# Two ends of a transformer kernel: inputs and modulation in halves ahead of the first product, and the last layer norm done with tokens on the partitions

## The chip, the cores and the metric

The kernel runs on one core of one Trainium2 chip. The metric is the device time of one execution in microseconds (us); the median of three runs stands for the kernel. The core has five engines with a queue each: TensorE (PE; its weight loads are shown as PEld), VectorE (DVE), ScalarE (ACT), GpSimd (POOL) and SyncE (SP), which issues all DMAs here. Data lies in SBUF with 128 partitions; PE writes to PSUM, eight banks of 128 x 512 f32.

## What is computed

One token sequence (512 tokens, 1024 features) goes through three layers. The first and the last of their parts matter here:

```python
mod = silu(c) @ w_mod + b_mod                    # 3 x 1024: shift, scale, gate
u = rms_norm(x, norm_w) * (1 + scale) + shift    # x: 512 x 1024
uc = rms_norm(ctx, norm_w) * (1 + scale_c) + shift_c   # 256 context tokens
p = u @ w_in                                     # then attention, conv, w_out
...
y = (silu(h @ w_gate) * (h @ w_up)) @ w_down     # 2816 wide
x = layer_norm(ALPHA * x + (1 + g_f) * y, ln_ffn_g, ln_ffn_b)   # the output
```

In between come two blocks with other attentions and two feed-forward parts. Everything is f32; the large products split both operands into a high part (F32R) and a low part and take three F32R matmuls instead of one f32 matmul.

## The kernel before

Every engine has its program written out by hand, and semaphores join them. The residual stream `xT` has features on the partitions: eight tiles of 128 features x 512 tokens. Weights come in chunks of 1 MB (`load_chunk`, two slots of `wraw`); ACT makes the high part (`split_high`, line 1453), DVE the low part (`split_low`, line 1952), and PE takes 16 blocks times three matmuls per chunk (`product`, lines 797 to 799). A chunk is loaded once the low part of the chunk two before is done.

**The prologue.** SP issues 15 small vectors, then the modulation weights of group 0 (four loads of 512 KB, called ticks), `x` (four loads), the context (1 MB), group 1, chunk 0, groups 2 and 3, nine small tables and chunk 1 (lines 486 to 515). A group is 512 columns of `w_mod`: groups 0 and 1 are the shift, groups 2 and 3 the scale. The 16 ticks go through four slots of `mfirst`; a load waits until PE has used the tick four before (line 480). PE multiplies each tick with the silu of the condition (`tick`, line 727), ACT copies a finished group to SBUF (`copy_group`, line 1461), PE transposes it (`turn_group`, line 740) and DVE adds the bias (`group_columns`, line 1960). PE also transposes `x` to `xT` (`input_tile`, tiles 0 to 7, line 762) and the normalized `x` (tiles 8 to 15). ACT makes the squares (line 1474), the root (line 1478) and the scaled copies (line 1482). When all four groups are there, DVE computes the scales (line 1985), splits chunk 0, and modulates tile by tile (line 1995); ACT makes the high part (line 1465) and DVE the low part (line 1968) of each. PE enters product 0 only behind the transposes of tile 15, and its k-th step waits for the k-th low part. Behind products 0, 1 and 2 PE transposes eight context tiles, and `ticks_of` puts two ticks of the next group behind each product; the group's turn lies in the middle of a later one (`TURN_AT`). On ACT the high parts of the context tiles come before `copy_group` (lines 1532 to 1535).

**The tail.** The last down projection has four column groups (j) of three chunks (c). DVE adds each finished pair of tiles to `xT` (`add_out`, line 2583). Mean and mean square come from matmuls with a matrix of 1/1024 (`moments`, lines 1223 to 1229), so they stand on all partitions at once; ACT squares tiles 4 to 7 late, and POOL sums (`far_half`). Then ACT copies the mean to SBUF (line 1758), DVE and POOL subtract it from the eight tiles (lines 2663 and 648), DVE and ACT compute the variance and its root (lines 2662, 1775, 1777), DVE multiplies the eight tiles (line 2670), ACT applies gain and bias (line 1788), PE transposes 32 blocks to PSUM (line 1426), DVE and ACT copy half token tiles to SBUF (lines 2878 and 1937), and SP stores them in eight DMAs of 256 KB (line 561).

Of the kernel before, what the change touches and what calls it, by code (L numbers as in the profile page):

```python
# [76 lines left out]
QUERY_AT = {5: 0, 6: 1, 7: 2, 8: 3}  # L77

# [66 lines left out]
def program(nc, t, out):  # L145
    ctx = ExitStack()
    with ctx:
# [8 lines left out]
        with ExitStack() as o:  # L156
# [80 lines left out]
        ln_pre, ln_m4, ln_sh, ln_pair, ln_six, ln_row, ln_v, ln_far, half_done = [sem(n) for n in (  # L237
            "ln_pre", "ln_m4", "ln_sh", "ln_pair", "ln_six", "ln_row", "ln_v", "ln_far", "half_done")]
# [8 lines left out]
        out_tile = sem("out_tile")  # L247
        fin_T, fin_v, fin_a = sem("fin_T"), sem("fin_v"), sem("fin_a")
# [207 lines left out]

        block = ctx.enter_context(nc.Block())
# [3 lines left out]
        def _(sp):  # L461
# [36 lines left out]
            for tt in range(TT):  # L498
                sp.dma_start(xtok[:, tt], t["x"][0, tt * P:tt * P + P, :]).then_inc(x_in, 16)
            sp.dma_start(ctok[:, :, :], t["ctx"][0].rearrange("(t p) n -> p t n", p=P)).then_inc(ctx_in, 16)  # L500
            for g in range(1, 4):
                for kp in range(4):
                    load_tick(g, kp)
                if g == 3:
                    sp.dma_start(ropet[:, 0], t["cos1"].rearrange("(t p) n -> p t n", p=P)).then_inc(tab_in, 16)
                    sp.dma_start(ropet[:, 1], t["sin1"].rearrange("(t p) n -> p t n", p=P)).then_inc(tab_in, 16)
                    sp.dma_start(qkw[:, 0], t["q_norm_w"].to_broadcast([P, HD])).then_inc(tab_in, 16)
                    for tt in range(TT):
                        sp.dma_start(posi[:, tt:tt + 1], t["positions_2"][0, tt * P:tt * P + P]
                                     .rearrange("(p o) -> p o", o=1)).then_inc(tab_in, 16)  # L510
                    sp.dma_start(ifr[:, :], t["inv2"].to_broadcast([P, 32])).then_inc(tab_in, 16)
                    sp.dma_start(qkw[:, 1], t["k_norm_w"].to_broadcast([P, HD])).then_inc(tab_in, 16)
                    load_chunk(1)
                if g == 1:
                    load_chunk(0)
# [37 lines left out]
            for n in range(N_DN[1], NCH - 2):  # L553
                load_chunk(n + 2)
            for i in range(2 * TT):
                tt, half = i % 4, i // 4
                if i < 6:
                    sp.wait_ge(fin_v, i + 1)
                else:
                    sp.wait_ge(fin_a, i - 5)  # L560
# [6 lines left out]
        def _(pool):  # L567
# [61 lines left out]
            def far_half(L, a):  # L629
# [70 lines left out]
        def _(pe):  # L700
# [45 lines left out]
            def input_tile(f):  # L746
# [4 lines left out]
                if f == 8:  # L751
                    pe.wait_ge(xn_rd, 4)
                if f == 16:
                    pe.wait_ge(xn_rd, 6)
# [10 lines left out]
            first_tiles = (range(0, 8), (), range(8, 11), ())  # L765
            for g in range(4):
                for kp in range(4):
                    tick(g, kp)
                if g >= 1:
                    turn_group(g - 1)  # L770
                for f in first_tiles[g]:
                    input_tile(f)
            turn_group(3)
            for f in range(11, 16):
                input_tile(f)

            def product(n, a, nk, u0, xh, xl, w_hi, w_lo, turn=None, k0=0, first=True, done=True, ready=u_lo, near=None, ends=None, mid=None):
# [8 lines left out]
                for i, (m, k) in enumerate(steps):  # L786
# [443 lines left out]

            def out_product(L, l, n0):
# [11 lines left out]
            def feed_forward(l):  # L1243
# [38 lines left out]
                moments(2 * l + 1, A_DN[l] + 3)  # L1282
# [140 lines left out]
            for k in range(KT):  # L1423
                pe.wait_ge(ax_rd, 32 + k + 1)
                for tt in range(TT):
                    last = tr(ps[:, 2 * tt + k // 4, (k % 4) * P:(k % 4) * P + P], xT[:, k, tt * P:tt * P + P], ident[:])
                    if k % 4 == 3:
                        last.then_inc(fin_T, 1)


        @block.scalar
        def _(act):
# [36 lines left out]
            act.wait_ge(ctx_in, 16)  # L1469
# [5 lines left out]
            copy_group(0)  # L1475
# [4 lines left out]
            for tt in range(6):  # L1480
                src = xtok[:, tt] if tt < 4 else ctok[:, tt - 4]
                A(xn[:, tt] if tt < 4 else ctok[:, tt - 4], src, ACT.Copy, scale=rstd[:, tt:tt + 1]).then_inc(xn_rd, 1)
            for g in range(1, 3):
                copy_group(g)
            split_high(0)
            copy_group(3)
            for i in range(8):
                high(U_U + i, uH[:, i])
            split_high(1)
# [9 lines left out]
            for n in range(N_PW):  # L1499
# [253 lines left out]
            def mean_row(L):  # L1753
                act.wait_ge(ln_mean, L + 1)
                if L < 3:
                    A(spare(L, 3), X[:, 0, :], ACT.Square).then_inc(ln_row, 1)
                else:
                    A(spare(L, 1), X[:, 0, :], ACT.Copy).then_inc(ln_row, 1)
# [13 lines left out]
            def norm(L, n):  # L1772
                rs = X[:, 2, :] if L < 3 else tmp[:, 0]
# [4 lines left out]
                if L < 3:  # L1778
                    for x in range(8):
                        i = U_LN[L] + x  # L1780
                        act.wait_ge(u_tmp, i + 1)
                        A(uH[:, x], tmp[:, i % 2], ACT.Identity, bias=fcol[:, L, 1, x:x + 1]).then_inc(u_hi, 1)  # L1782
                        if x == 2:
                            act.wait_ge(chunk_done, n - 1)
                            split_high(n)
                for x in range(8):
                    act.wait_ge(ln_t, 16 * L + x + (5 if L == 3 else 9))
# [8 lines left out]
            def feed_forward(l):  # L1796
# [15 lines left out]
                for n in range(N_DN[l], N_DN[l] + 12):  # L1812
                    L, a = 2 * l + 1, A_DN[l] + 3
                    if n == N_DN[l] + 11:
                        nc.scalar.preload_act_table_set(LOG_EXP)
                        squares(L, a, (6, 7))
                        mean_row(L)
# [8 lines left out]
                norm(2 * l + 1, N_ODD + 1)  # L1826
# [108 lines left out]
            for tt in range(2, TT):  # L1935
                act.wait_ge(fin_T, 4 + tt + 1)
                A(otok[:, tt, 512:D], ps[:, 2 * tt + 1, :], ACT.Copy).then_inc(fin_a, 1)


        @block.vector  # L1940
        def _(dve):
# [13 lines left out]
            def group_columns(g):  # L1955
                dve.wait_ge(modT, g + 1)
                if g < 6:
                    o, b = mod1[:, 4 * g:4 * g + 4, :], cols[:, VBM + 4 * g:VBM + 4 * g + 4]
# [17 lines left out]
            V.reciprocal(rstd, rstd).then_inc(rin_rd, 1)  # L1976
            dve.wait_ge(cols_rd, 1)
            for g in range(2):
                group_columns(g)
            for g in range(2, 4):  # L1980
                group_columns(g)
            dve.wait_ge(mod_rd, 4)

            for c, dst in ((0, scS), (1, scC)):
                V.scalar_tensor_tensor(dst, mod1[:, 8:16, c], 1.0, cols[:, VNW:VNW + 8], ALU.add, ALU.mult)\
                    .then_inc(sc_rd, 1)
            split_low(0)
            dve.wait_ge(sc_rd, 2)
# [9 lines left out]
            for i in range(8):  # L1998
                modulate(i)
                if i >= 1:  # L2000
# [654 lines left out]
            def last_norm(L):  # L2655
                row, sq, var = spare(L, 1), spare(L, 3), spare(L, 2)
                dve.wait_ge(ln_row, L + 1)
                link(V.tensor_tensor(sq, row, row, ALU.mult))
                for x in range(4):
                    if x == 1:  # L2660
                        dve.wait_ge(ln_var, L + 1)
                        V.tensor_tensor(var, X[:, 1, :], sq, ALU.subtract).then_inc(ln_v, 1)
                    V.tensor_tensor(xT[:, x], xT[:, x], row, ALU.subtract).then_inc(ln_t, 1)
                dve.wait_ge(ln_rs, 2 * L + 2)
                for x in range(8):
                    if x < 4:
# [248 lines left out]
```

## Time and profile before

| what | value |
|---|---|
| median of 3 runs (lowest, highest) | 1800.19 us (1798.35, 1802.16) |
| the profiled execution's own time | 1807.2 us |
| its span in the trace | 1805.5 us |
| mean granted clock of PE | 0.964 of full |
| busy share of PE, DVE, ACT, POOL | 93%, 56%, 37%, 19% |

Matmuls are pipelined and their ends are modelled, so two of them overlap in the rows; the distance from start to start is what one takes in a row of its kind. A row of the timeline that says x4 has merged four neighbours. An f32 matmul stands as two passes.

### The profile page before, as it was taken

To read this page: it belongs to the slowest core of one execution; us is meant where nothing else is said; L and a number is where in the kernel's file an instruction comes from. 1 tells how busy PE (TensorE), PEld (TensorE's weight loads), DVE (VectorE), ACT (ScalarE), POOL (GpSimd) and SP (SyncE) were. 2 spreads that over 40 slices of the span, in tenths; PEclk is the share of its full clock that TensorE was granted. 3 is DMA by queue.
4 is the path that set the end of the run, shared out by engine and by line. 5 is a ranking of instruction groups with operands and counts; after the bars stand their busy time and mean duration, and the time that the engine had idled before them with its cause. 6 is when DMAs were issued, how large, how long until landed. Compare 5 with 4: busy or idle time off the path is not lost.

```text
span 1805.5 us, 22686 instructions
## 1 busy us (share of the span) xinstructions
PE 1677.7 (93%) x8899; PEld 1371.9 (76%) x8905; DVE 1017.3 (56%) x1430; ACT 665.1 (37%) x896; POOL 341.7 (19%) x264
## 2 busy tenths in 40 slices
PE   4899999999998998999999999899979899999996
PEld 3698787888776876788887876677758688888875
DVE  1558798677879657633333246756675733333244
ACT  4313465443353433433332223434453533333123
POOL 0000000000000002688885011224311100000012
PEclk8899999999998899999999999999989999999999
DMA  8535300242222233466664222212002223322221
GB/s 287 181 107 172 104 25 1 88 163 94 94 82 82 70 94 117 140 185 186 186 186 134 87 95 85 82 59 71 24 24 71 68 95 102 106 93 87 87 82 47
DMA packets 145349, 187.08 MB, mean 104 GB/s; under 512 B 6893, under 2 KB 104533, under 8 KB 145268
## 3 DMA queue, kind: packets, MB, share of 16 engines
q1 hardware_dynamic: 145268, 185.96, 32.4%
q8 instruction: 55, 0.90, 0.2%
q14 instruction: 26, 0.21, 0.0%
HBM read 183.85 MB, written 2.10 MB: 103 GB/s over the span
## 4 chain that ended last, share of the span: by engine, by line
PE 58%; DVE 16%; POOL 9%; issue 7%; DMA 5%; ACT 4%; SPq 0%; another core or an unknown queue 0%; POOLq 0%; DVEq 0%; ACTq 0%
PE ps L797 7%; PE ps L799 7%; PE ps L798 7%; POOL mraw L598 4%; POOL msum L605 4%; DMA mraw<-in_w_mod_dram 3%; PE ps L1260 2%; PE ps L1267 2%; PE ps L1261 2%; PE ps L1268 2%; PE ps L1264 2%; PE ps L1269 2%; PE ps L1315 2%; PE ps L1317 2%; PE ps L1316 2%
## 5 line engine op out<-in xcount | busy, mean ns | idle before, releaser
L1453 ACT ACTIVATE whi<-wraw 128x2048 fp32r<-128x2048 f32 x71 | 135.8, 1913 | 313.4 <-PE ps L799 231.6
L1952 DVE TENSOR_TENSOR wlo<-wraw,whi 128x2048 fp32r<-128x2048 f32 x64 | 148.9, 2327 | 174.4 <-ACT whi L1453 174.2
L2689 DVE TENSOR_TENSOR wlo<-wraw,whi 128x2048 fp32r<-128x2048 f32 x22 | 51.6, 2347 | 203.4 <-ACT whi L1804 203.4
L1260 PE MATMUL ps<-uH,whi 128*128 128x512 f32 x352 | 141.0, 401 | 10.6 <-ACT uH L1782 8.3
L797 PE MATMUL ps<-hH,whi 128*128 128x512 f32 x352 | 141.2, 401 | 0.0
L798 PE MATMUL ps<-hL,whi 128*128 128x512 f32 x352 | 140.0, 398 | 0.0
L799 PE MATMUL ps<-hH,wlo 128*128 128x512 f32 x352 | 140.0, 398 | 0.0
L1261 PE MATMUL ps<-uH,wlo 128*128 128x512 f32 x352 | 139.4, 396 | 0.0
L1268 PE MATMUL ps<-uL,whi 128*128 128x512 f32 x352 | 136.9, 389 | 0.0
L1269 PE MATMUL ps<-uH,wlo 128*128 128x512 f32 x352 | 136.9, 389 | 0.0
L1267 PE MATMUL ps<-uH,whi 128*128 128x512 f32 x352 | 136.9, 389 | 0.0
L1264 PE MATMUL ps<-uL,whi 128*128 128x512 f32 x352 | 111.0, 397 | 3.9 <-DVE uL L2630 3.9
L605 POOL TENSOR_TENSOR msum<-msum,mraw 128x512 f32<-128x512 f32 x66 | 107.6, 1630 | 5.2
L797 PE MATMUL ps<-uH,whi 128*128 128x512 f32 x256 | 103.3, 403 | 0.0
L798 PE MATMUL ps<-uL,whi 128*128 128x512 f32 x256 | 100.7, 393 | 0.0
L799 PE MATMUL ps<-uH,wlo 128*128 128x512 f32 x256 | 100.7, 393 | 0.0
L598 POOL TENSOR_TENSOR mraw<-mraw,cpad 128x1024 f32<-128x1024 f32 x44 | 84.2, 1912 | 56.5 <-PE ps L734 43.7
L1808 ACT ACTIVATE whi<-wraw 128x2048 fp32r<-128x2048 f32 x22 | 42.2, 1920 | 137.3 <-PE ps L1269 137.3
L1801 ACT ACT_TABLE_LOAD x22 | 28.2, 1283 | 173.3 <-PE ps L1264 173.3
L2012 DVE SCALAR_TENSOR_TENSOR cy<-utp,cols,cy 128x512 f32<-128x512 f32 x116 | 87.1, 751 | 3.4
L1260 PEld LDWEIGHTS ps<-uH,whi 128*128 128x128 f32 x352 | 67.8, 193 | 26.9 <-issue 13.0
L632 POOL TENSOR_TENSOR sqd<-sqd 128x512 f32<-128x512 f32 x2 | 2.8, 1386 | 435.2 <-ACT sqd L1751 435.2
(488 smaller groups left out, 3945.3 us busy)
## 6 DMA issues: line engine op xcount, KB each, us to landing
mraw<-in_w_mod_dram SPq DMA_DIRECT2D x104, 512.0 KB, 3.7
wraw<-in_w_gate_dram SPq DMA_DIRECT2D x22, 1024.0 KB, 5.3
wraw<-in_w_up_dram SPq DMA_DIRECT2D x22, 1024.0 KB, 5.4
wraw<-in_w_down_dram SPq DMA_DIRECT2D x16, 1024.0 KB, 5.2
wraw<-in_w_in_dram SPq DMA_DIRECT2D x11, 1024.0 KB, 5.3
mfirst<-in_w_mod_dram SPq DMA_DIRECT2D x16, 512.0 KB, 7.3
wraw<-in_w_in_even_dram SPq DMA_DIRECT2D x8, 1024.0 KB, 5.2
wraw<-in_w_in_odd_dram SPq DMA_DIRECT2D x16, 512.0 KB, 4.5
```

The source lines that it names most:

```text
L598: g.tensor_tensor(w, w, cpad[:, 2 * kp:2 * kp + 2, 2:3].to_broadcast([P, 2, GW]), ALU.mult).then_inc(msum_rd, 1)
L605: g.tensor_tensor(msum[:], msum[:], w[:, kk], ALU.add).then_inc(msum_rd, 1)
L797: mm(o, h, xh[:, k0 + k], start=(first and k == 0), stop=False)
L798: mm(o, h, xl[:, k0 + k], start=False, stop=False)
L799: last = mm(o, l, xh[:, k0 + k], start=False, stop=(done and k == nk - 1))
L1260: mm(o[m], w_[0][m][:, k], uH[:, k], start=(k == 0), stop=False)
L1261: mm(o[m], w_[1][m][:, k], uH[:, k], start=False, stop=False)
L1264: last = mm(o[m], w_[0][m][:, k], uL[:, k], start=False, stop=(k == KT - 1))
L1267: mm(o[m], w_[0][m][:, k], uH[:, k], start=(k == 0), stop=False)
L1268: mm(o[m], w_[0][m][:, k], uL[:, k], start=False, stop=False)
L1269: last = mm(o[m], w_[1][m][:, k], uH[:, k], start=False, stop=(k == KT - 1))
L1952: V.tensor_tensor(wlo[:, n % 2, :], wraw[:, n % 2, :], whi[:, n % 2, :].bitcast(F32), ALU.subtract).then_inc(lo_done, 1)
```

## The change

In the prologue the loads are put in the order `x`, group 0, context, chunk 0, groups 1, 2 and 3, chunk 1, tables. `FIRST_GROUPS` makes group 1 the first half of the scale and group 2 the second half of the shift, so tiles 0 to 3 need groups 0 and 1 alone. Scales are computed in two halves. PE transposes tiles 0 to 3 ahead of the first ticks, and puts the last two ticks, tiles 13 to 15 and the last turn into product 0. ACT splits chunk 0 ahead of the root; DVE takes one of the four scaled copies. For products with context tiles ACT's `copy_group` comes before the high parts.

In the tail the last layer norm isn't applied to `xT`. PE multiplies blocks of `xT` (as the stationary operand) with diagonal blocks that hold the gain, which gives gain times x with tokens on the partitions, and subtracts mean times gain by matmuls with one row (high and low parts: three of them per half token tile). The moments are also computed as columns, one per token tile. DVE multiplies each PSUM bank by the root's column and adds the bias, which a DMA has spread over all partitions, and SP stores.

```diff
+FIRST_GROUPS = (0, 2, 1, 3, 4, 5)
@@ SP
-                c0 = GW * (g if g < 6 else (g - 6) % 12)
+                c0 = GW * (FIRST_GROUPS[g] if g < 6 else (g - 6) % 12)
...
+            for tt in range(TT):
+                sp.dma_start(xtok[:, tt], t["x"][0, tt * P:tt * P + P, :]).then_inc(x_in, 16)
             for kp in range(4):
                 load_tick(0, kp)
             sp.dma_start(ctok[:, :, :], t["ctx"][0].rearrange("(t p) n -> p t n", p=P)).then_inc(ctx_in, 16)
+            load_chunk(0)
             for g in range(1, 4):
                 for kp in range(4):
                     load_tick(g, kp)
+            load_chunk(1)
...
+                if n == N_DN[1] + 3:
+                    sp.wait_ge(mod_rd, 30)
+                    sp.dma_start(biasB, t["ln_ffn_b_2"][1:2, :].to_broadcast([P, D])).then_inc(fin_in, 16)
+                    sp.wait_ge(h_lo, 23)
+                    sp.dma_start(gain_row, t["ln_ffn_g_2"][1:2, :]).then_inc(fin_in, 16)
@@ POOL, far_half
-                if L == 3:
-                    pool.wait_ge(ln_row, L + 1)
-                    for x in range(4, 8):
-                        g.tensor_tensor(xT[:, x], xT[:, x], spare(L, 1), ALU.subtract).then_inc(ln_far, 1)
@@ PE, prologue
+            for f in range(4):
+                input_tile(f)
+            ticks(0)
+            for f in range(4, 8):
+                input_tile(f)
+            turn_group(0)
+            ticks(1)
+            turn_group(1)
+            for f in range(8, 11):
+                input_tile(f)
+            ticks(2)
+            turn_group(2)
+            input_tile(11)
+            ticks(3, (0,))
+            input_tile(12)
+            ticks(3, (1,))
+
+            def between(k):
+                if k == 1:
+                    ticks(3, (2, 3))
+                    input_tile(13)
+                if k == 2:
+                    input_tile(14)
+                    turn_group(3)
+                if k == 4:
+                    input_tile(15)
...
+                    if n == 0 and m == 0:
+                        between(k)
@@ PE, tail
+            def token_tiles(i, k0):
+                for k in range(k0, k0 + 4):
+                    mm(ps[:, last_bank(i), (k - k0) * P:(k - k0) * P + P], xT[:, k, (i % 4) * P:(i % 4) * P + P],
+                       gain_diag[:, k], start=(k == k0), stop=False, skip_group_check=True)
+
+            def less_mean(i):
...
+                mm(o, mean_h[:, ts], gain_h[:, c], start=False, stop=False, skip_group_check=True)
+                mm(o, mean_h[:, ts], gain_l[:, c], start=False, stop=False, skip_group_check=True)
+                mm(o, mean_l[:, ts], gain_h[:, c], start=False, stop=True, skip_group_check=True).then_inc(fin_T, 1)
+
+            def last_moments(a):
+                one = onesD[:, 0:1]
+                def column(src, c, start, stop):
+                    for tt in range(TT):
+                        last = mm(X[:, 1, c + tt:c + tt + 1], src[:, tt * P:tt * P + P], one, start=(start and tt == 0),
+                                  stop=stop, skip_group_check=True)
+                    return last
...
+                mm(X[:, 0, :], onesD[:], spare(3, 0), start=True, stop=False)
+                column(spare(3, 0), 4, True, False)
...
+                column(square(3, 0), 0, False, False)
+                acc_tile(pe, a, 1)
+                mm(X[:, 0, :], onesD[:], xT[:, 7], start=False, stop=True).then_inc(ln_mean, 1)
+                column(xT[:, 7], 4, False, True)
+                pe.wait_ge(ln_sq, 32)
+                column(square(3, 7), 0, False, True).then_inc(ln_var, 1)
+                token_tiles(4, 4)
+                token_tiles(5, 4)
+                pe.wait_ge(fin_g, 2)
+                pe.wait_ge(fin_ml, 1)
+                less_mean(0)
+                less_mean(1)
+                token_tiles(6, 4)
+                less_mean(2)
+                less_mean(3)
+                pe.wait_ge(ln_v, 4)
+                token_tiles(7, 4)
+                for i in range(4, 8):
+                    less_mean(i)
@@ PE, feed_forward, ahead of the last chunk
+                        if l and j == 3 and c == 2:
+                            pe.wait_ge(fin_dg, 1)
+                            acc_gone(pe, a - 1)
+                            for i in range(4):
+                                token_tiles(i, 0)
@@ ACT
             for tt in range(6):
...
+                if tt == 4:
+                    copy_group(0)
+                    act.wait_ge(ctx_in, 16)
...
+            split_high(0)
             act.wait_ge(ssq_rd, 6)
             act.wait_ge(rin_rd, 1)
             A(rstd, rstd, ACT.Sqrt).then_inc(rstd_rd, 1)
...
+            for tt in range(3):
+                A(xn[:, tt], xtok[:, tt], ACT.Copy, scale=rstd[:, tt:tt + 1]).then_inc(xn_rd, 1)
+            copy_group(1)
             for i in range(8):
                 high(U_U + i, uH[:, i])
+                if i in (1, 2):
+                    copy_group(1 + i)
+                if i == 3:
+                    for tt in range(2):
+                        A(ctok[:, tt], ctok[:, tt], ACT.Copy, scale=rstd[:, 4 + tt:5 + tt]).then_inc(xn_rd, 1)
...
+                if 3 in ticks_of(n):
+                    copy_group(group_of(n))
                 for f in CTX_TILES.get(n, ()):
                     high(f - 8, ucH[:, f - 16])
-                if 3 in ticks_of(n):
-                    copy_group(group_of(n))
...
+            def last_root_steps():
+                act.wait_ge(ln_mean, 4)
+                A(mean_h, X[0:1, 0, :], ACT.Copy, scale=-1.0).then_inc(fin_mh, 1)
+                act.wait_ge(ln_var, 4)
+                A(last_sq, X[:, 1, 4:8], ACT.Square).then_inc(ln_row, 1)
+                act.wait_ge(ln_v, 4)
+                A(last_root, last_var, ACT.Ln, bias=eps2).then_inc(ln_rs, 1)
+                act.wait_ge(ln_rs, 7)
+                A(last_root, last_root, ACT.Exp, scale=-0.5).then_inc(ln_rs, 1)
@@ DVE
+            split_low(0)
+            dve.wait_ge(rstd_rd, 1)
+            V.tensor_scalar(xn[:, 3], xtok[:, 3], rstd[:, 3:4], None, ALU.mult).then_inc(xn_v, 1)
...
             for i in range(8):
+                if i == 4:
+                    low(3, uL[:, 3], uH[:, 3])
+                    scales(1)
                 modulate(i)
...
+            def last_norm():
+                dve.wait_ge(fin_mh, 1)
+                V.scalar_tensor_tensor(mean_l, X[0:1, 0, :], -1.0, mean_h.bitcast(F32), ALU.mult, ALU.subtract).then_inc(fin_ml, 1)
+                dve.wait_ge(ln_row, 4)
+                V.tensor_tensor(last_var, X[:, 1, 0:4], last_sq, ALU.subtract).then_inc(ln_v, 1)
+                dve.wait_ge(ln_rs, 8)
+                for i in range(2 * TT):
...
+                    V.scalar_tensor_tensor(otok[:, tt, half], ps[:, last_bank(i), :], last_root[:, tt:tt + 1], biasB[:, half],
+                                           ALU.mult, ALU.add).then_inc(fin_v, 1)
...
+                        if l and j == 2 and c == 2:
+                            for k in range(KT):
+                                last = V.tensor_scalar(gain_diag[:, k], ident[:], cols[:, VLFG + 8 + k:VLFG + 9 + k], None, ALU.mult)
```

## Rows read from the trace of the kernel before

**Rows 1.** The page's head and its first part: span, busy time of the engines.

```profile
span 1805.5 us, 22686 instructions
PE 1677.7 (93%) x8899; PEld 1371.9 (76%) x8905; DVE 1017.3 (56%) x1430; ACT 665.1 (37%) x896; POOL 341.7 (19%) x264
```

**Rows 2.** Chain of waits ahead of product 0: start us, us, what.

```profile
39.54 6.17 DMA mfirst<-in_w_mod_dram
...
47.90 2.20 DVE wlo L1952
...
57.34 0.43 PE ps L797
```

**Rows 3.** Timeline of SP, then single issues with us to landing.

```profile
8.51 2.09 SPq L499 DMA_DIRECT2D xtok<-in_x_dram  x4
...
19.49 1.53 SPq L472 DMA_DIRECT2D wraw<-in_w_in_dram  x1
28.46 11.45 SPq L483 DMA_DIRECT2D mfirst<-in_w_mod_dram  x8
...
xtok<-in_x_dram SPq DMA_DIRECT2D x1, 512.0 KB, 12.0
...
wraw<-in_w_in_dram SPq DMA_DIRECT2D x1, 1024.0 KB, 13.6
...
mfirst<-in_w_mod_dram SPq DMA_DIRECT2D x1, 512.0 KB, 6.2
```

**Rows 4.** Timeline of the prologue: ACT, PE and DVE pieces that the sum uses.

```profile
31.71 1.28 ACT L1478 ACT_TABLE_LOAD   x1 [0.34 <-DVE small L1976]
...
33.24 4.27 ACT L1482 ACTIVATE xn<-xtok,small 128x1024 f32<-128x1024 f32 x4
...
40.07 2.72 PE L762 MATMUL ps<-ident,xn 128*128 128x128 f32 x12
...
53.84 0.81 DVE L1995 TENSOR_SCALAR tmp<-ps,small,mod 128x512 f32<-128x512 f32 x1
54.57 0.68 DVE L1968 TENSOR_TENSOR uL<-tmp,uH 128x512 fp32r<-128x512 f32 x1
```

**Rows 5.** Timeline around product 2's first group; last, a stretch by engine.

```profile
82.31 1.91 ACT L1453 ACTIVATE whi<-wraw 128x2048 fp32r<-128x2048 f32 x1 [2.73 <-PE ps L799]
...
82.78 1.08 PE L727 MATMUL ps<-mraw,cpad 128*32 128x128 f32 x32
...
90.40 0.48 PE L740 MATMUL ps<-ident,msum 128*128 128x128 f32 x1 [3.47 <-ACT msum L1461]
...
90.40:100.90 10.50, 10.50 (x75) 10.50 (x76) 3.88 (x8) 0.01 (x1) 0.00 (x0) 0.84 0.09 30
```

**Rows 6.** Chain (first row) and timeline of the tail.

```profile
1781.28 0.23 PE ps L797
...
1777.89 0.75 DVE L2583 SCALAR_TENSOR_TENSOR xT<-ps,g1p,xT 128x512 f32<-128x512 f32 x1 [9.77 <-PE ps L799]
...
1781.82 1.02 PE L1223 MATMUL ps<-spd,onesD 128*128 128x512 f32 x2
1782.67 1.02 PE L1225 MATMUL ps<-sqd,onesD 128*128 128x512 f32 x2
...
1798.23 4.48 SPq L561 DMA_DIRECT2D out_dram<-otok  x8
...
1798.52 0.42 PEld L1426 LDWEIGHTS ps<-ident,xT 128*128 128x128 f32 x4 [0.28 <-ACT xT L1788]
```

**Rows 7.** Timeline of PE: f32 matmuls in other stages (two passes each).

```profile
517.07 0.38 PE L1091 MATMUL ps<-spt,negone 128*128 128x128 f32 x2
517.29 0.39 PE L1091 MATMUL ps<-spt,negtri 128*128 128x128 f32 x2
...
888.92 0.95 PE L734 MATMUL ps<-small,msum 128*128 128x1 f32 x8
889.73 0.48 PE L1260 MATMUL ps<-uH,whi 128*128 128x512 f32 x1
```

More of the change, by code:

```diff
@@ L1281, in feed_forward @@
                                 ends=2 * l + 1 if j == 3 and c == 2 else None)
-                moments(2 * l + 1, A_DN[l] + 3)
+                if l == 0:
+                    moments(1, A_DN[0] + 3)
+                else:
+                    last_moments(A_DN[1] + 3)
             feed_forward(0)
@@ L1420, in _ @@
             feed_forward(1)
[L1423 to L1428, printed above, removed]
         @block.scalar
@@ L1754, in mean_row @@
                 act.wait_ge(ln_mean, L + 1)
[L1755 to L1758, printed above, removed]
+                A(spare(L, 3), X[:, 0, :], ACT.Square).then_inc(ln_row, 1)
             def out_steps(L, n0):
@@ L1772, in norm @@
             def norm(L, n):
-                rs = X[:, 2, :] if L < 3 else tmp[:, 0]
+                rs = X[:, 2, :]
                 act.wait_ge(ln_v, L + 1)
@@ L1777, in norm @@
                 A(rs, rs, ACT.Exp, scale=-0.5).then_inc(ln_rs, 1)
[L1778 to L1785, printed above, removed]
-                for x in range(8):
-                    act.wait_ge(ln_t, 16 * L + x + (5 if L == 3 else 9))
+                for x in range(8):
+                    i = U_LN[L] + x
+                    act.wait_ge(u_tmp, i + 1)
+                    A(uH[:, x], tmp[:, i % 2], ACT.Identity, bias=fcol[:, L, 1, x:x + 1]).then_inc(u_hi, 1)
+                    if x == 2:
+                        act.wait_ge(chunk_done, n - 1)
+                        split_high(n)
+                for x in range(8):
+                    act.wait_ge(ln_t, 16 * L + x + 9)
                     A(xT[:, x], xT[:, x], ACT.Identity, bias=fcol[:, L, 3, x:x + 1],
                       scale=fcol[:, L, 2, x:x + 1]).then_inc(ax_rd, 1)
+            def last_root_steps():
[7 more added lines that the diff above has]
+                A(last_root, last_root, ACT.Exp, scale=-0.5).then_inc(ln_rs, 1)
             act.wait_ge(ds_rd, NS)
@@ L1825, in feed_forward @@
                         squares(L, a, (4, 5))
-                norm(2 * l + 1, N_ODD + 1)
+                    if l and n == N_DN[l] + 8:
+                        act.wait_ge(fin_in, 32)
+                        A(gain_h, gain_row, ACT.Copy).then_inc(fin_g, 1)
+                if l == 0:
+                    norm(1, N_ODD + 1)
+                else:
+                    last_root_steps()
             feed_forward(0)
@@ L1976, in _, with scales @@
             V.reciprocal(rstd, rstd).then_inc(rin_rd, 1)
+            split_low(0)
+            dve.wait_ge(rstd_rd, 1)
+            V.tensor_scalar(xn[:, 3], xtok[:, 3], rstd[:, 3:4], None, ALU.mult).then_inc(xn_v, 1)
             dve.wait_ge(cols_rd, 1)
[L1978 to L1988, printed above, removed]
+            def scales(half):
+                for g in (2 * half, 2 * half + 1):
+                    group_columns(g)
+                dve.wait_ge(mod_rd, 2 * half + 2)
+                k = slice(4 * half, 4 * half + 4)
+                for c, dst in ((0, scS), (1, scC)):
+                    V.scalar_tensor_tensor(dst[:, k], mod1[:, 8 + 4 * half:12 + 4 * half, c], 1.0,
+                                           cols[:, VNW + 4 * half:VNW + 4 * half + 4], ALU.add, ALU.mult).then_inc(sc_rd, 1)
+                dve.wait_ge(sc_rd, 2 * half + 2)
+            scales(0)
             def modulate(i):
@@ L2653, in norm @@
                     V.tensor_tensor(xT[:, x], xT[:, x], R, ALU.mult).then_inc(ln_t, 1)
[L2655 to L2666, printed above, removed]
-                        dve.wait_ge(ln_t, 16 * L + 4)
-                    else:
-                        dve.wait_ge(ln_far, x - 3)
-                    V.tensor_tensor(xT[:, x], xT[:, x], tmp[:, 0], ALU.mult).then_inc(ln_t, 1)
+            def last_norm():
[5 more added lines that the diff above has]
+                for i in range(2 * TT):
+                    tt, half = i % 4, slice(512 * (i // 4), 512 * (i // 4) + 512)
+                    dve.wait_ge(fin_T, i + 1)
+                    V.scalar_tensor_tensor(otok[:, tt, half], ps[:, last_bank(i), :], last_root[:, tt:tt + 1], biasB[:, half],
+                                           ALU.mult, ALU.add).then_inc(fin_v, 1)
             mixer_low(0)
@@ L2874, in _ @@
             feed_forward(1)
-            for i in range(6):
-                tt, half = i % 4, i // 4
-                dve.wait_ge(fin_T, i + 1)
-                V.tensor_copy(otok[:, tt, half * 512:half * 512 + 512], ps[:, 2 * tt + half, :]).then_inc(fin_v, 1)
 _INS = ["x", "c", "ctx", "c_ctx", "w_mod", "b_mod", "norm_w", "w_in", "q_norm_w", "k_norm_w", "conv_w", "conv_b",
```

96 lines of the change are left out of this document (46 added, 50 removed).

## The prediction, made before the changed kernel was run

> **What bounds the kernel now.** I read the page first, then the chain of waits at both ends of the run, then the timelines there. The page says that TensorE (PE) has matmuls in flight for 93% of the span [rows 1], so only stretches in which PE waits are worth time. There are three here. All times are us from the start of the span.
>
> The prologue: the chain up to the first product is made of `w_mod` transfers; the last of the 16 holds it from 39.5 to 45.7, then DVE splits the first weight chunk (2.2 us, 47.9 to 50.1) before it can modulate the first tile, and product 0 starts behind the last transposes, at 57.3 by the chain [rows 2]. With 48 matmuls it ends near 69.3.
> The first turned group of product 2: PE stands 3.5 us for a copy by ACT that waits behind three context copies [rows 5].
> The tail: the last down projection gives way to the moments at 1781.8, and then come a row of DVE and ACT passes over eight tiles, transposes, copies and eight stores; the span ends at 1805.5, which is 23.7 us [rows 1, 6].
>
> **Prologue, step by step.** Where do the bytes land? `x`'s last transfer, issued at 10.1, lands 12.0 later (22.1); chunk 0, issued at 19.5, lands 13.6 later (33.1). Between them lie the context, the second group and chunk 0, four MB: 2.75 us per MB [rows 3]. With that rate and the new order (x, group 0, ctx, chunk 0, group 1): x at 16.6, group 0 at 22.1, ctx 24.9, chunk 0 27.6, group 1 33.1. The loads are issued early enough, since PE frees the four slots from about 20 on.
>
> ACT then has a chain: split of chunk 0 (1.9, to 29.5), root with table load (1.28 and six columns, to 31.0), three scaled copies at 1.07 (to 34.2), the copy of group 1 (0.3) [rows 4, 5]. The fourth scaled copy and the split's low part move to DVE, which is idle there; the chunk's 2.2 us leave the chain. Turn and columns take under 1 us (35.4), the first tile's transposes 0.9 (12 took 2.72) [rows 4], so the first modulation starts near 36 and not 50.1. That head start can't be kept whole: now groups 2 and 3 decide. PE does tiles 8 to 10 before the ticks of group 2, and the loads of group 3 wait for those ticks: issued from about 38.2, the bus empty, they land at 42.3 to 46.3 by 1.3 us each and an issue to landing of 4 to 6 [rows 3], hardly other than the 45.7 of before. So half of product 0 (k 0 to 3) is what is put beside the wait. PE: group 2 done 39.8, turn, tiles 11 and 12 and two ticks to 44, k=0 (six matmuls, 1.4) to 45.8, last ticks 46.6, tile 13, k=1, tile 14, turn of group 3 at about 49.7. ACT's third high part waits in front of k=3 behind the copy of group 3, which waits for the last tick: ready at 49.7, in time. Scales 50.5; from there DVE needs 1.5 us per tile (0.81 + 0.68) [rows 4] and PE 1.4 per k, so k=7 ends near 50.5 + 1.6 + 4 x 1.5 + 1.4 = 59.5, where it was 69.3. Chunk 1's parts now come late: high part after the last high copy (58.4), low part 60.7, while PE is busy with context tiles and ticks to 61.2. Term: **-9.8**. Bounds: -6 if PE has the half clock through the first half, 1.2 GHz, at which the chain gives a matmul 0.43 [rows 2] where it gives 0.23 late in the run [rows 6]; -12 if group 3's loads land 2 sooner.
>
> SP: the nine table loads go behind chunk 1, their issuing now stands before chunk 2. At half a us each, as `x`'s four took 2.09 [rows 3], that is 5 us: chunk 2 is issued at about 47 and its parts are needed at the end of product 1, past 70. Cost nothing; the cover is product 1.
>
> **Context copies.** With the group's copy ahead of three context copies it follows the split of chunk 3 (to 84.2) and is ready 2 us before PE asks at 86.7. Saved: the 3.5 us, and the slow clock after it: the stretch behind the stall has a granted clock of 0.84 over 10.5 us [rows 5], of which 1.4 us are lost. Term: **-4.9**, bounds -3.5 and -5. DVE's next copy waits for the end of product 2 either way, so I see nothing late in its place, unless its conv taps fill the room. The context tiles lose 0.3, hidden.
>
> **Tail.** Ahead of the last chunk PE gets 16 matmuls of 128x128 f32 with the gain on the diagonal. One such matmul takes 0.22, start to start [rows 7]; 16 x 0.22 = 3.5, all on the path, since PE is full there: **+3.5**. The diagonal (eight DVE passes of 128x128), the gain's high and low part, the bias (512 KB) and the gain row lie in the down projection, where DVE, ACT and the queue wait for PE; nothing, unless they took longer than a chunk's product, 48 x 0.23 = 11 us, leaves beside the 1.9 and 2.3 us of the next weight split.
> Behind the last chunk, on the old axis: two moment matmuls remain (0.85 each [rows 6]), the two over squares become columns, and the mean also gets columns: 4 groups of 4 matmuls with one moving column. A group of four took 0.81 [rows 7]. 1781.8 + 1.7 + 3.2 = 1786.8. Then 16 more diagonal matmuls (3.5) and 24 of one row by 512 in F32R, taken at the 0.23 of the products [rows 6]: 5.5. PE ends at 1795.8. Root (a few columns on ACT and DVE, under 1.2 us) and the high and low part of the mean hide behind the first of these. DVE follows each half tile with one pass of 0.75 [rows 6]: last at 1796.8, its issue to 1797.3, and the landing. The old end came 2.8 after the last issue ended, at 1802.7 [rows 1, 6]; 2.4 without a queue in front: 1799.7, plus 3.5 is 1803.2 against 1805.5. Term: **-2.3**. Gone are the row copy, both subtractions (DVE and POOL together), eight multiplications, eight ACT passes and the eight stores' crowding. Bounds: between -5 (columns and one-row matmuls at 0.1) and +3 (columns at 0.4, the one-row matmuls at 0.3).
> The diagonal matmuls take the place of transposes, whose weights load in 0.42 for four [rows 6], 0.11 each; the f32 matmul's 0.22 [rows 7] is twice that.
> The Trainium skill, page "TensorE: Matmul & The Clock Gate", section Terms, says that the transpose mode is four times as fast for FP32; by that rule the 32 would cost 0.44 each, 7 us more, and this tail would lose 5 rather than gain. The trace has the very shape at 0.22 [rows 7], so I take that.
>
> **Sum.** -9.8 - 4.9 - 2.3 = -17.0. Nothing between takes it up: each later stage starts from PE's progress and not from a fixed time. The profiled execution took 1807.2 (span 1805.5); it would become 1790.2. The median of the runs is 1800.19, 7 below the profiled one, and I subtract the same: **1783.2**.
>
> **Rivals.**
> 1. The forecast, 1783.2. Chance 0.60.
> 2. Group 3 or the clock holds product 0: the last tick comes 4 to 5 us later, because its load waits for a tick behind tiles 8 to 10, and low part, scales and modulation follow it in line. For it: the 6.2 us from issue to landing of the last load while the bus was not full [rows 3]. Against: four loads are under way at once. 1783.2 + 5 = 1788.2. Chance 0.22.
> 3. The diagonal matmuls cost 0.44: 1783.2 + 7 = 1790.2. For it only the doubling from a transpose to an f32 matmul [rows 6, 7]. Chance 0.07. The skill's rule is this case.
> 4. The reordered copies do nothing, because the copy then waits for something else (the ticks' last transfer): 1788. Against: PE had done the ticks at 83.9 [rows 5]. Chance 0.05.
> 5. Slower. Place: the four slots of `mfirst`. ACT's high part 2 stands behind the copy of group 2, high part 3 behind that of group 3, and each load behind a tick. If this turned the ring into one load at a time, groups 2 and 3 would need 8 x (6.2 + 0.6) = 54 us from 33 on, to 87, and product 0 would end at 100, 31 later than before: 1800.2 + 31 - 7.2 = 1824. It decides once the last load lands later than 63 (46.3 + 17). Against: before, the same ring brought a load each 1.3 us. Chance 0.03.
> That all three parts cancel for other reasons gets 0.03.
>
> **How the numbers follow.** The time is that of case 1. Its own bounds (-6 to -12, -3.5 to -5, +3 to -5, not all at an end together) give 1778 to 1789; with cases 2 to 4 the range reaches to 1791. Under 2 in 10 stays outside. A measurement of this kernel tells 0.2%, 3.6 us, from no change: faster 0.94, same 0.02, slower 0.04.
>
> **What would show it.** Right: first modulation at about 36, last `mfirst` matmul near 46.5, product 0 done at 58 to 61; no wait of L740's matmul at product 2; f32 diagonal matmuls in pairs of passes 0.11 apart; from last product matmul to end 18 (23.7 before), after 3.5 more ahead of it. Wrong: a wait for `mfirst` past 48, a gap in front of product 1 over 1 us, a half clock in the tail, or DVE's last passes bunched behind the root.

## The result, and the profile after

The changed kernel takes a median of **1793.4 us**, where the kernel before beside it takes 1801.4; the ratio is 0.9946 [0.9926, 0.9967], a gain of 9.7 us with an interval of 5.9 to 13.3. Faster, as forecast, but by little more than half of the 17.0, and outside the range of 1778 to 1791. Taken once more (c_after below), the gain was 5.0 us, with an interval of 0.9 to 9.2.

The page's head of the kernel after, answering to [rows 1]:

```profile
span 1796.4 us, 22850 instructions
PE 1690.3 (94%) x8989; PEld 1383.6 (77%) x8989; DVE 1010.4 (56%) x1430; ACT 657.0 (37%) x887; POOL 335.6 (19%) x260
```

PE is busy 12.6 us longer in a span that is 9.1 shorter. That alone says that waits went and matmul time came. Where? First the prologue: SP, ACT, DVE and PE timelines of the kernel after, answering to [rows 2 to 4] (start us, us, what):

```profile
21.22 19.54 SPq L500 DMA_DIRECT2D mfirst<-in_w_mod_dram  x12
...
27.40 1.91 ACT L1533 ACTIVATE whi<-wraw 128x2048 fp32r<-128x2048 f32 x1 [0.80 <-DMA wraw<-in_w_in_dram]
30.86 3.23 ACT L1563 ACTIVATE xn<-xtok,small 128x1024 f32<-128x1024 f32 x3
48.19 0.28 ACT L1541 ACTIVATE msum<-ps 128x128 f32<-128x128 f32 x1 [7.89 <-PE ps L740]
...
35.74 1.53 DVE L2091 TENSOR_SCALAR tmp<-ps,small,mod 128x512 f32<-128x512 f32 x2 [0.49 <-PE ps L776]
58.31 2.29 DVE L2044 TENSOR_TENSOR wlo<-wraw,whi 128x2048 fp32r<-128x2048 f32 x1 [1.11 <-ACT whi L1533]
...
47.05 1.08 PE L740 MATMUL ps<-mfirst,cpad 128*32 128x128 f32 x32
50.38 0.27 PE L753 MATMUL ps<-ident,msum 128*128 128x128 f32 x1
59.11 0.39 PE L834 MATMUL ps<-uH,wlo 128*128 128x512 f32 x1
```

Chunk 0 is there at 27.4, the first modulation starts at 35.7, the last ticks end at 48.1, the turn of group 3 is at 50.4 and product 0 ends at 59.5. The second place is product 2's first group, answering to [rows 5]:

```profile
75.06 0.26 ACT L1541 ACTIVATE msum<-ps 128x128 f32<-128x128 f32 x1
...
77.70 0.27 PE L753 MATMUL ps<-ident,msum 128*128 128x128 f32 x1
```

The copy is made 2.4 us before PE turns it at 77.7, with no idle time ahead of the turn. The third is the tail, answering to [rows 6]. The chain, from the matmuls ahead of the last chunk on (start us, us, what):

```profile
1756.93 3.57 PE ps L1268 x32
...
1774.39 3.62 PE ps L1268 x16
...
1780.44 0.43 PE ps L1275
1780.87 2.00 PE ps L1268 x8
...
1793.19 0.75 DVE otok L2763
```

And its timeline and windows (window; us; then busy time and instructions of PE, PEld, DVE, ACT, POOL; granted clock; DMA share; GB/s):

```profile
1768.74 1.02 PE L1288 MATMUL ps<-spd,onesD 128*128 128x512 f32 x2
1769.60 0.95 PE L1282 MATMUL ps<-onesD,spd 128*128 128x1 f32 x8
...
1774.25 3.76 PE L1268 MATMUL ps<-mraw,xT 128*128 128x128 f32 x16
...
1778.54 0.62 PE L1274 MATMUL ps<-uL,wlo 1*128 1x512 f32 x1
```

```profile
1754.00:1768.70 14.70, 14.70 (x81) 12.54 (x80) 0.75 (x1) 1.92 (x2) 2.55 (x2) 1.00 0.01 1
1768.70:1774.20 5.50, 5.50 (x37) 4.50 (x36) 1.43 (x2) 1.22 (x2) 0.00 (x0) 0.95 0.00 0
1774.20:1793.00 18.80, 18.80 (x57) 14.42 (x57) 5.42 (x8) 0.68 (x3) 0.00 (x0) 0.50 0.22 84
```

This is what to see: the clock falls near the end of the moments, at 1773.6, with PE busy for 5.50 of 5.50 us. Behind them PE is busy for all 18.8 us of the last window, and yet the granted clock there is 0.50, which is 1.2 GHz. A matmul with one row (its two operands lie on one partition) takes 0.43 from start to start, and eight passes over the diagonal, which are four matmuls, take 2.0. From the first moment to the end it is 27.7 us, where it was 23.7 [rows 1, 6] and 17.9 was forecast. The 32 passes (16 matmuls) over the diagonal ahead of the last chunk add 3.5, as forecast: the lead over the kernel before falls from 16.6 us to 13.1 across them.

### The profile page after: what moved, and what is told of

Read it like the earlier page. It is cut to its first block, busy times and chain, and to the rows that moved or that the text cites. A ratio compares the mean times of both kernels' runs of the same rounds, so it can differ in the third digit from the quotient of the medians.

```text
span 1796.4 us, 22850 instructions
## 1 busy us (share of the span) xinstructions
PE 1690.3 (94%) x8989; PEld 1383.6 (77%) x8989; DVE 1010.4 (56%) x1430; ACT 657.0 (37%) x887; POOL 335.6 (19%) x260
## 4 chain that ended last, share of the span: by engine, by line
PE 60%; DVE 14%; POOL 9%; issue 7%; DMA 5%; ACT 4%; SPq 1%; POOLq 0%; DVEq 0%; ACTq 0%
PE ps L832 7%; PE ps L834 7%; PE ps L833 7%; POOL mraw L615 4%; POOL msum L622 4%; DMA mraw<-in_w_mod_dram 3%; PE ps L1340 2%; PE ps L1347 2%; PE ps L1349 2%; PE ps L1341 2%; PE ps L1344 2%; PE ps L1348 2%; PE ps L1403 2%; PE ps L1405 2%; PE ps L1404 2%
```

## The experiments

I took the changed kernel apart first (parts alone), then varied the tail's matmuls. The question behind the parts was whether the tail gives back what the front wins.

**e_swap**: the copies' order alone, on the kernel before.

```
+                if 3 in ticks_of(n):
+                    copy_group(group_of(n))
                 for f in CTX_TILES.get(n, ()):
                     high(f - 8, ucH[:, f - 16])
-                if 3 in ticks_of(n):
-                    copy_group(group_of(n))
```

> The kernel before with one edit: on ACT the copy of a group comes ahead of the context tiles' high parts (one place decides, product 1). By the forecast the 3.5 us stall of PE in product 2 and about 1 us of slow clock behind it go: -4.4 us (the changed kernel's trace has product 2 end 14.2 earlier, product 0 only 9.9). Rival: the time is taken up again before the end, 0 us.

Measured: 0.9979 [0.9963, 0.9995], 3.8 us. Timeline of ACT and PE of e_swap:

```profile
83.95 0.26 ACT L1461 ACTIVATE msum<-ps 128x128 f32<-128x128 f32 x1
...
86.59 0.27 PE L740 MATMUL ps<-ident,msum 128*128 128x128 f32 x1
```

The turn that stood until 90.4 [rows 5] comes at 86.6, 3.8 us sooner, and the slow clock behind it is gone too: from the context tiles ahead of product 2 to those behind it (81.85 to 95.34) PE takes 13.5 us, where it took 18.7 (82.03 to 100.69). The context tiles of before, then of e_swap:

```profile
82.03 0.82 PE L762 MATMUL ps<-ident,ctok 128*128 128x128 f32 x6
...
100.69 0.60 PE L762 MATMUL ps<-ident,ctok 128*128 128x128 f32 x4
...
81.85 0.82 PE L762 MATMUL ps<-ident,ctok 128*128 128x128 f32 x6
...
95.34 0.60 PE L762 MATMUL ps<-ident,ctok 128*128 128x128 f32 x4
```

That is 5.2 by the trace; the interval of the runs is 0.9 to 6.7 us. The rival, nothing left of it at the end, is out, if narrowly.

**e_prologue**: the new prologue alone (tokens first, halves of modulation, the fourth scaled copy and low part on DVE). Its edit is the prologue's part of the diff.

```
+            for tt in range(TT):
+                sp.dma_start(xtok[:, tt], t["x"][0, tt * P:tt * P + P, :]).then_inc(x_in, 16)
             for kp in range(4):
                 load_tick(0, kp)
...
+            load_chunk(0)
             for g in range(1, 4):
...
             for i in range(8):
+                if i == 4:
+                    low(3, uL[:, 3], uH[:, 3])
+                    scales(1)
                 modulate(i)
```

> The kernel before with the new prologue alone (loads, halves, order on PE, ACT and DVE), the copies' order and the tail as before. If product 0 ends 9.9 earlier and nothing takes it up: -9.9 us. Rival: part of it is lost in the stages after, -5 us or less.

Measured: 0.9932 [0.991, 0.9954], 12.2 us, with 9.9 inside the interval (8.3 to 16.2) and the rival's 5 outside. Its waits still have the stall of product 2, as they should with the old order of the copies (engine, line, waited for: us in total, times, longest):

```profile
PE ps L741 <- ACT msum L1484: 3.5, 1, 3.5
```

**e_tail**: the new tail alone. One thing must be said of it: the copies' order was not in it, though the expectation says that it was; the kernel had the old prologue and the old order. So the theory's number for it is the tail's +7.5 alone, and the forecast's is -2.3.

```
+                        if l and j == 3 and c == 2:
+                            pe.wait_ge(fin_dg, 1)
+                            acc_gone(pe, a - 1)
+                            for i in range(4):
+                                token_tiles(i, 0)
...
-                moments(2 * l + 1, A_DN[l] + 3)
+                if l == 0:
+                    moments(1, A_DN[0] + 3)
+                else:
+                    last_moments(A_DN[1] + 3)
```

> The kernel before with the new tail (and the copies' order, 4.4 us, that lies in the same stretch of the difference). Theory: the tail costs, as in the changed kernel's trace, 27.7 us from the first moment matmul to the end against 23.7, and 3.5 us ahead of the last chunk, so +7.5 us for the tail and +3 us with the copies' order. Rival, my forecast: the tail gains 2.3, so -6.7 us together, and the missing time is elsewhere.

Measured: 1.0031 [1.0014, 1.0049], 5.6 us slower (2.5 to 8.8); the 7.5 is inside, the gain of 2.3 is not. Its tail starts at 1786.6 and the span ends at 1814.2, 27.6 us. Timeline of e_tail:

```profile
1786.57 1.02 PE L1265 MATMUL ps<-spd,onesD 128*128 128x512 f32 x2
...
1797.23 0.62 PE L1250 MATMUL ps<-uL,wlo 1*128 1x512 f32 x1
```

The tail by itself makes the kernel slower; nothing of the prologue is needed for that.

**e_front**: prologue and copies' order, with the tail of before: the two diffs of e_prologue and e_swap together.

> The changed kernel with the tail of before: new prologue and copies' order. If the parts add up: -14.3 us against before, which is 6 to 7.5 us better than the changed kernel. Rival, that the prologue's gain is not real at the end: -9 us, as the changed kernel.

Measured: 0.9912 [0.9892, 0.9933], 15.8 us, where the two terms of the forecast say 14.7. Its tail takes 24.0 (from 1762.9 to 1786.9). So the whole change loses 6 us against this part of it. The intervals of the two ratios just overlap; it is e_tail that shows the loss by itself.

**The tail's matmuls.** Two theories for the half clock were left: the thin matmuls bring it (one moving column in the statistics, one row in the three terms of mean times gain), or it is there whatever they move (then filling them gives nothing). The next three kernels fill them without changing what is computed.

**e_cols64**: the 16 column matmuls move 64 columns of ones instead of one.

```
-                one = onesD[:, 0:1]
+                one = onesD[:, 0:64]
-    last = mm(X[:, 1, c + tt:c + tt + 1], ...
+    last = mm(X[:, 1, 64 * (c + tt):64 * (c + tt) + 64], ...
```

(The readers take every 64th column.)

> The changed kernel, but each of the 16 column matmuls moves 64 equal columns instead of one (only the first is read). Theory (the clock falls since one-column and one-row matmuls keep little of the array at work): the granted clock stays at full past 1774, up to the one-row matmuls at least, and the tail of 27.7 us shortens by 2 to 4 us; it may then fall in the one-row part. Rival 1 (the clock falls with the product's end, whatever follows): clock and tail as in the changed kernel, 0 us. Rival 2 (clock is not the matter, the number of matmuls is): no gain, rather some 0.5 us lost.

**e_rows128**: the one-row matmuls contract over 128 rows. The gain's other 127 rows are zero, so the result stays; the mean stands on all 128.

```
-  gain_h = uL[0:1, 0:2, :]...
-  mean_h, mean_l = wlo[0:1, ...
+  gain_both = uL[:, 0:4, :]...
+  mean_h, mean_l = wlo[:, ...
+  V.memset(gain_both.bitcast(F32), 0.0).then_inc(fin_dg, 1)
```

> The changed kernel, but the mean and gain rows stand in tiles of 128 partitions, the gain's other 127 rows zero: the 24 one-row matmuls use all rows of the array, same count, same result. Theory: the clock, fallen in the columns, comes back to full within the 128-row stretch from about 1778 on, matmuls there 0.23 instead of 0.43: 4 to 6 us less. Rival 1: stays at half, 0 us. Rival 2: 0 us.

**e_full_array**: both, the diffs of e_cols64 and e_rows128 together.

> Both edits: 64 moving columns and 128 rows. Theory: no low use of the array anywhere in the tail, clock full throughout, tail near the 18 us of my forecast, 8 to 10 us less than the changed kernel. Rivals 1 and 2: 0 us.

Measured, all beside the same runs of the kernel before:

| kernel | ratio | median, us | tail, us | from : to |
|---|---|---|---|---|
| after | 0.9946 [0.9926, 0.9967] | 1793.4 | 27.7 | 1768.7 : 1796.4 |
| e_cols64 | 0.9946 [0.9926, 0.9966] | 1788.2 | 21.9 | 1762.8 : 1784.7 |
| e_rows128 | 0.9924 [0.9899, 0.995] | 1784.4 | 19.4 | 1763.5 : 1782.9 |
| e_full_array | 0.9917 [0.99, 0.9934] | 1784.3 | 17.8 | 1765.3 : 1783.1 |

(The kernel after is from its own comparison, not from this one.) The ratios alone don't tell these apart, and that of e_cols64 shows no gain over the kernel after; the tail in each trace does, by 5.8, 8.3 and 9.9 us. The tail of the kernel after repeats well: 27.7, 27.6 and 27.6 in three traces (with e_tail and c_after); each filled form has one trace here. e_cols64, columns as above:

```profile
1762.80:1769.90 7.10, 7.10 (x53) 6.06 (x51) 1.59 (x3) 1.89 (x5) 0.00 (x0) 1.00 0.00 0
1769.90:1775.90 6.00, 6.00 (x30) 4.55 (x28) 2.84 (x4) 0.00 (x0) 0.00 (x0) 0.88 0.35 129
1775.90:1781.40 5.50, 5.50 (x13) 3.76 (x12) 2.25 (x3) 0.00 (x0) 0.00 (x0) 0.50 0.39 146
```

e_rows128, with the last 0.2 us ahead of its first matmul with 128 rows, and that matmul:

```profile
1763.50:1768.90 5.40, 5.40 (x37) 4.43 (x36) 1.44 (x2) 1.23 (x2) 0.00 (x0) 0.96 0.00 0
1768.90:1772.10 3.20, 3.20 (x17) 3.20 (x18) 0.16 (x1) 0.68 (x3) 0.00 (x0) 0.54 0.00 0
1772.10:1779.70 7.60, 7.59 (x43) 6.22 (x41) 4.88 (x7) 0.00 (x0) 0.00 (x0) 1.00 0.42 159
...
1771.90:1772.10 0.20, 0.20 (x4) 0.20 (x4) 0.00 (x0) 0.00 (x0) 0.00 (x0) 1.00 0.00 0
...
1772.13 0.48 PE L1273 MATMUL ps<-uL,wlo 128*128 128x512 f32 x1
```

e_full_array:

```profile
1765.30:1770.50 5.20, 5.20 (x37) 4.24 (x36) 1.44 (x2) 1.23 (x2) 0.00 (x0) 1.00 0.00 0
1770.50:1779.90 9.40, 9.34 (x58) 7.96 (x57) 5.11 (x9) 0.68 (x3) 0.00 (x0) 1.00 0.35 131
```

With 64 columns the clock stays through the statistics and falls later, among the one-row matmuls (at 1774.4). With 128 rows alone it falls in the one-column matmuls as before (at 1768.4). With both it never falls. So each thin form brings the fall by itself: the columns by e_rows128 against e_full_array, the rows by e_cols64 against e_full_array.

The return of the clock in e_rows128 is another matter. The expectation saw it come within the 128-row stretch, but it came at 1771.8, inside the eight diagonal matmuls that end ahead of the first matmul with 128 rows (1772.13); that is why the mean of that window is 0.54 and not 0.50. The same eight matmuls in the kernel after, at 1774.2 to 1777.9, ended at the half clock. So the filled rows are not shown to bring the clock back. What is shown is that it stayed at 1.00 through all 24 of them, where with one row it fell (e_cols64), and part of the short tail of e_rows128 may be luck of this one execution.

The same instruction at the two clocks, from the timelines of e_cols64:

```profile
1770.51 0.39 PE L1275 MATMUL ps<-uL,wlo 1*128 1x512 f32 x1
...
1776.98 0.62 PE L1275 MATMUL ps<-uL,wlo 1*128 1x512 f32 x1
```

(The times in the rows run to the modelled end; start to start it is 0.23 and 0.43.) And e_full_array's tail of 17.8 is the forecast's 17.9: the instruction counts and the order of the sum were right, its clock was not.

**e_pack64**: with 64 moving columns, the three one-row matmuls of a half tile become one: gain high, low, high on rows 0, 32, 64 of a tile that is zero elsewhere, against the mean's high, high and low part.

```
-  mm(o, mean_h[:, ts], gain_h[:, c], ...)
-  mm(o, mean_h[:, ts], gain_l[:, c], ...)
-  mm(o, mean_l[:, ts], gain_h[:, c], start=False, stop=True, ...)
+  mm(o, mean3[:, ts], gain3[:, c], start=False, stop=True, ...)
```

> The changed kernel with one matmul per half token tile for the mean instead of three: high and low parts on partitions 0, 32 and 64 of a tile of 128, all other rows of the gain zero; and 64 moving columns. 16 matmuls fewer. Theory: at full clock 16 x 0.23 = 3.7 us less than e_full_array on PE, though the eight DVE passes and the stores then bound the end, so 9 to 12 us less than the changed kernel. Rival 2 (count, not clock): 16 x 0.43 = 7 us less, with the clock at half.

Measured: 0.9892 [0.9874, 0.9909], 19.4 us faster than the kernel before; the tail is 15.6 us, 12.1 less than in the kernel after, where 9 to 12 were expected. The clock stays at 1.00, so the rival (the count of matmuls, at a half clock) is out. Windows and timeline of e_pack64:

```profile
1767.00:1772.20 5.20, 5.20 (x37) 4.24 (x36) 1.44 (x2) 1.23 (x2) 0.00 (x0) 1.00 0.00 0
1772.20:1777.90 5.70, 5.67 (x42) 4.98 (x41) 3.49 (x7) 0.68 (x3) 0.00 (x0) 1.00 0.30 112
```

```profile
1774.57 5.37 DVE L2764 SCALAR_TENSOR_TENSOR otok<-ps,small,mraw 128x512 f32<-128x512 f32 x8 [1.78 <-PE ps L1273]
...
1775.35 4.95 SPq L578 DMA_DIRECT2D out_dram<-otok  x8
```

PE is no longer last. DVE's eight passes run without a gap from 1774.6 to 1779.9, and each store is issued behind its pass: what bounds the end has gone from PE to DVE, 0.67 a pass.

**c_after, c_front, c_pack64**: the kernel after, e_front and e_pack64 once more, side by side, without a further edit, since their ratios came from different comparisons.

> The changed kernel once more, beside the two versions below on the same chip. -7 to -10 us against before.

> New prologue and copies' order with the tail of before, as e_front: -14 to -16 us.

> As e_pack64. By its trace the tail takes 15.6 us and 3.7 more ahead of the last chunk, 19.3 against the 23.7 of before: 4.4 us better than c_front and about 12 better than c_after, so -18 to -21 us against before. Rival (tail no better than the old one at full clock): equal to c_front.

Measured: 0.9972 [0.9949, 0.9995], 0.9938 [0.9918, 0.9958] and 0.9917 [0.9892, 0.9941], medians 1794.3, 1787.0 and 1782.6. As gains that is 5.0, 11.2 and 15.0 us, where 7 to 10, 14 to 16 and 18 to 21 were expected: all three missed, each by 2 to 3 us and to the same side. So a gain against the kernel before shifts by some 5 us from one comparison to the other, and the order of the three is what repeats. The first moment of c_after is this row, its span ends at 1789.8, so its tail is 27.6 again:

```profile
1762.17 1.02 PE L1288 MATMUL ps<-spd,onesD 128*128 128x512 f32 x2
```

The granted clock of c_after falls in the same place, 0.95 over 1762.1 to 1767.6 and 0.50 over the 18.9 us behind. The ratio of after less that of front is 0.0034 both times, 6 us for the new tail (the trace says 27.7 + 3.5 - 23.7 = 7.5). The ratio of c_pack64 is 0.0021 below that of c_front, 3.8 us; the traces say 15.6 + 3.5 against 23.8, 4.7. The intervals of these two overlap, so the order rests on the traces, and the times agree with it. Against c_after, the gap of c_pack64 is clear: 0.0055, 9.9 us. Its tail is 15.6 again (1761.9 to 1777.5), with the granted clock at 1.00 until PE is done.

## Why the prediction was right or wrong

**Prologue, forecast -9.8: right.** Product 0 ends at 59.5, forecast 59.5, before 69.3. The steps hold too: chunk 0 at 27.4 (27.6), scaled copies until 34.1 (34.2), first modulation 35.7 (36), low part of chunk 1 ready 60.6 (60.7). The last ticks came 1.5 late (48.1 for 46.6) and the turn of group 3 0.7 late. That was made good for another reason than forecast: PE ran from 48.1 to 59.3 without a gap (11.20 of 11.20 us), where the sum had the last k wait for DVE, whose last low part was done at 57.2. Two errors met there, and to hit 59.5 was partly luck: in the ten traces with this prologue product 0 ends between 58.3 and 61.0. The way of the bytes (us per MB from two landings, then the new order laid out by it) gave chunk 0 to 0.2 us. Rival 2, the clock or group 3 holding it by 4 to 5 us, is out; the half clock did come, around the start of product 0, but only from 43.1 to 46.4. Rival 5 is out too: the 12 `mfirst` issues are over at 40.8.

**Table loads, forecast nothing: 0.8.** Issuing the nine tables took from 41.3 to 50.9 and not 5 us; chunk 2 was issued at 51.0 for the forecast 47, and behind it the first ticks of group 4. The second of them is then what PE waits for ahead of product 1:

```profile
51.44 1.43 SPq L500 DMA_DIRECT2D mraw<-in_w_mod_dram  x2
...
61.36 0.65 PE L740 MATMUL ps<-mraw,cpad 128*32 128x128 f32 x16 [0.63 <-DMA mraw<-in_w_mod_dram]
```

From product 0's end to product 1's start PE takes 2.60 us, where it took 1.76. Such a wait is in three of the ten traces with this prologue. No run moves the tables, so that they are the cause is argued.

**Context copies, forecast -4.9: right.** The start of what follows product 2 comes 14.3 sooner than before: 9.9 from product 0, less the 0.8, plus 5.2 from product 2, which takes 13.5 us with its context tiles and ticks where it took 18.7. e_swap has the same 5.2 in its trace and 3.8 in its runs. The stall of 3.5 and the slow clock behind it (priced at 1.4) both went. Rival 4 is out.

**The middle, forecast 0: not resolved.** The lead over the kernel before was 14.5 us at 300, 13.2 at 520 to 650, 15.8 at 1140 and 16.6 from 1340 on. In the trace of c_after, the same kernel, it was 15.2 at 300 and 23.2 from 1340 on. So two executions differ by more than 6 us there, and a change of 2 or 3 us in the middle can't be seen in one trace; it is part of why single spans differ from medians (the profiled 1805.5 of before was high).

**Tail, forecast -2.3: wrong, +7.5 by the trace, +5.6 in the runs of e_tail.** The step that failed is the price of the tail's matmuls. It read "16 more diagonal matmuls (3.5) and 24 of one row by 512 in F32R, taken at the 0.23 of the products [rows 6]: 5.5". Measured: the 16 took 3.62 + 2.0 + 2.0 = 7.6, and the 24 took the rest of the 18.8 between 1774.4 and 1793.2, 11.2. That is 4.1 and 5.7 over, with 0.6 more in the moments, less 0.6 at the end: the 9.8 by which 27.7 misses 17.9. Both prices were right at full clock, as e_full_array shows with 17.8 and e_cols64 with its 0.23 for one row, and both came from rows where matmuls of full shape stand around them. In the tail they stand among 16 matmuls with one moving column and 24 with one row. I had named the half clock in the tail as a sign of error, and given it neither a term nor a rival; the bound of +3 covered less than half of the 7.5. The tail had no row for a one-row matmul (it went by the products', with 128 rows), one row for a single group of one-column matmuls, and none for the sequence; the chance of 0.60 did not say so.

**Rival 3 (0.44 for a diagonal matmul) would have given a number close to the result for a wrong reason.** Its 1790.2 lies near 1793.4, and the 16 matmuls in the tail did take 0.45 to 0.5 each. But the 16 ahead of the last chunk, the same instruction, took 3.57 at the granted clock 1.00, 0.22 each, with full products around them. It is the clock, not the form. The rule of the Trainium skill that I weighed against the row (page "TensorE: Matmul & The Clock Gate", section Terms) is not borne out at full clock: the row's 0.22 was the right price.

**The sum.** Measured terms: -9.9 + 0.8 - 5.2 + 7.5 = -6.8, against -9.1 in the spans; the 2.3 between them are what the lead grew in the middle. The runs say -9.7 [5.9 to 13.3] and, once more, -5.0 [0.9 to 9.2].

What stays open is why these forms lower the clock, and what brings it back. Nothing was run between one column and 64, or between one row and 128; e_pack64 has three rows of values, but contracts over 128 rows too.

## What to carry to other kernels

Price an instruction from a row whose neighbours are like those it will have, and ask of a new stretch what clock it will be granted, even if PE has no gap in it: the same matmul cost 0.23 and 0.43 here. Where a change trades vector passes for many thin matmuls (one column, one row), try to fill their rows and columns, or pack several of them into one, as the three terms went into one matmul here. And time the parts apart: a gain of 9.7 hid one of 15.8 (e_front) and a loss of 5.6 (e_tail).

## What the runs showed of the hardware that was not expected

The granted clock fell from 1.00 to 0.50 in a stretch where PE was busy for 5.50 of 5.50 us, and stayed there for 18.80 of 18.80 busy us. I had taken the clock to follow idle gaps, as behind the stall of product 2 [rows 5]. What PE did before the fall was 16 matmuls with one moving column and two passes of a full moment matmul between them; with 64 moving columns the clock was still 1.00 at that place. Among the one-row matmuls of e_cols64 it fell at 1774.4; with 128 rows in use it stayed at 1.00, although 127 of the gain's rows were zeros.

The Trainium skill, page "TensorE: Matmul & The Clock Gate", section "Part 1: The HAM clock gate", says that the clock is set by how busy PE has been, with half as the state of an idle PE. By the profile's busy time that rule alone would have kept the full clock here; the measurement decides, and matmuls that move one column or contract over one row did not keep it.

A second point is small: 64 moving columns cost nearly what one costs. At full clock the eight passes of four matmuls take 1.00 with 64 columns in e_cols64, where they take 0.95 with one; start to start it is 0.84 and 0.81.

```profile
1763.63 1.00 PE L1282 MATMUL ps<-onesD,spd 128*128 128x64 f32 x8
```
